# A two-block transformer kernel: stick-breaking attention computed transposed, and products joined around the last norm turns

## The chip, the cores and the metric

The kernel runs on one core of a Trainium2 chip. The metric is the time of one execution on the device in microseconds (us), as the median of three runs. Smaller is better.

## What is computed

The reference is a first block (a state-space and linear-attention mixer with a mixture of experts) on a sequence of 512 rows of width 1024, and behind it a block that is applied twice with different weights (layers l = 0 and 1). The change lies in that second block, all in float32:

```python
h = _rms_norm(x, attn_norm[l]); proj = h @ w_in[l]           # 7328 columns
o_a, o_b = dilated attention, latent attention
o_c = _stick_breaking_attention(c_q, c_k, c_v)                # 8 heads of 64
merged = gates0 * (o_a @ wb_a) + gates1 * (o_b @ wb_b) + gates2 * (o_c @ wb_c)
x = x + merged @ w_out[l]
h2 = _rms_norm(x, mlp_norm[l])
x = x + square(relu(h2 @ w_ff1[l])) @ w_ff2[l]
```

Stick-breaking attention of one head is, with `z` the scaled scores and `strict` the mask key < query:

```python
log_one_minus = where(strict, log_sigmoid(-z), 0.0)
after = cumsum(log_one_minus, reverse=True) - log_one_minus   # over the later keys
weights = exp(where(strict, log_sigmoid(z) + after, -inf))
out = weights @ v
```

So each weight needs the sum of softplus(z) over all keys from its own up to the query.

## The kernel before

Every engine has its own program, written out by hand, and waits on counted semaphores ("lines"). A product of two float32 matrices that must be precise is made of three products of rounded parts (`three`): each operand is split into a high part, written rounded by ScalarE, and a low part, the rest, written by GpSimd (`part_gpsimd`) or VectorE. Helper lines: L229 is every product of TensorE, L232 every transpose, L240 to L256 VectorE's operations, L291 ScalarE's.

A layer of the second block goes through these stages, with a meeting of all four engines (`meet`: each drains, adds to its end line and waits for those of all) between them:

- The norm of x and its turn: per tile of 128 rows ScalarE squares, VectorE scales (`xn`), TensorE turns with 8 transposes (`nturn`), VectorE multiplies with the gain, ScalarE writes the high part and VectorE the low part (`hT`, or `hs` ahead of the feed-forward). For l = 0 this stands at the end of the mixture of experts (`moe_*`), for l = 1 at the end of the feed-forward of l = 0. Then comes a meeting, and only then the first product (`tok a0`).
- An order written by `block2_order`, a list of steps that all engines walk in the same order. Lanes of attention steps are woven with dense products ("filler"). The last piece is the stick stage, between the meetings B and C: 32 units (8 heads by 4 query tiles) in six lanes, five steps each, with the 48 steps of the gate products d = 4 to 7 as filler. A gate step is 6 products of 128x512.
- A unit of the stick stage with `nk` = 128 to 512 keys, queries on the partitions: score on TensorE; scale and mask on VectorE; Abs, Exp, Ln on ScalarE; maximum and addition and then a scan from the last key down on VectorE (L3304); a subtraction on GpSimd (L3709); Exp on ScalarE; `nk`/128 transposes of the weights on TensorE; a copy out of PSUM; the products with v; a copy. GpSimd also writes the low parts of the gate weights (L2620).
- The merge: o_a, o_b, o_c are turned, then for d = 0 to 7 three branch products, sigmoid of the gates (read back from DRAM, `gad`), multiplications and additions on VectorE. SyncE's queue issues in its order: gates 0 and 1, the two output weights (`in_b0o`, 2 MB each), then for each d the branch weights and the gates, each behind a wait. Then the output projection and the norm turns of the feed-forward, a meeting, and the feed-forward (`f1`, `f2`).

## Time and profile before

| | us |
|---|---|
| median of 3 runs | 4967.44 (4967.3 to 4972.65) |
| the profiled execution | 4978.45 |
| its span | 4976.6 |
| TensorE busy | 4460.7 (90%) |
| VectorE, ScalarE, GpSimd busy | 2113.1, 1495.0, 792.0 |
| mean granted clock of TensorE | 0.943 |

A span is the time from the first to the last instruction of the profiled execution. "Idle before" is the time in which an engine did nothing ahead of an instruction, and the arrow names what released it. The granted clock is the share of 2.4 GHz that TensorE had.

### The profile page before, as it was taken

The numbers are of one execution on the slowest core, as the hardware profiler recorded it, in microseconds if no ns is written. First come the engines' busy times: TensorE is split into PE (matmuls) and PEld (weight loads), VectorE is DVE, ScalarE is ACT, GpSimd is POOL, SyncE is SP. The second block draws the span as 40 slices with busy tenths as digits, with TensorE's granted clock in tenths as the row PEclk, the third lists the DMA queues.
The fourth block names the chain that finished last, engine by engine and source line by source line (L and its number), as shares of the span: only waits on it lengthen the run. The fifth ranks groups of instructions, "written<-read, shape, count | busy, mean of one in ns | idle before, by whom it ended". The sixth has DMA issues, their size and how long they took to land. (4 is left out here: it accounts for less than half of the span.)

```text
span 4976.6 us, 90377 instructions
## 1 busy us (share of the span) xinstructions
PE 4460.7 (90%) x38676; PEld 3119.2 (63%) x38676; DVE 2113.1 (42%) x3803; ACT 1495.0 (30%) x2632; POOL 792.0 (16%) x499
## 2 busy tenths in 40 slices
PE   6899899988998899979999798978999988878999
PEld 3566666666555554465443776757788866656787
DVE  2555554554355552131111446354443446345343
ACT  2343333332222221010000334453232334443232
POOL 0021111110132230000000221243000321333000
PEclk9899999988999999989999899989999999999999
DMA  6200000000110123427999311214222211214221
GB/s 228 71 28 11 17 19 17 5 24 16 43 43 29 48 87 131 154 107 302 405 403 411 122 63 50 69 49 168 88 98 77 94 56 48 69 61 154 98 102 51
DMA packets 86824, 512.05 MB, mean 103 GB/s; under 512 B 10504, under 2 KB 11032, under 8 KB 45848
## 3 DMA queue, kind: packets, MB, share of 16 engines
q1 hardware_dynamic: 86424, 506.28, 26.9%
q8 instruction: 305, 5.00, 0.4%
q14 instruction: 95, 0.78, 0.0%
HBM read 476.85 MB, written 29.38 MB: 102 GB/s over the span
## 5 line engine op out<-in xcount | busy, mean ns | idle before, releaser
L229 PE MATMUL ps<-rounded,rounded 128*128 128x512 f32 (+2 forms) x7968 | 1660.4, 367 | 44.3 <-DVE rounded L240 23.7
L229 PEld LDWEIGHTS ps<-rounded,rounded 128*128 128x128 f32 x7968 | 1338.1, 193 | 302.8 <-issue 36.1
L229 PE MATMUL ps<-lower 128*128 128x512 f32 (+10 forms) x4976 | 1075.0, 393 | 56.3 <-issue 22.8
L229 PE MATMUL ps<-upper 64*64 64x64 f32 (+8 forms) x15584 | 834.2, 259 | 152.0 <-DVE upper L268 38.2
L291 ACT ACTIVATE upper<-ps 128x512 f32<-128x512 f32 (+6 forms) x953 | 440.2, 491 | 1671.0 <-PE ps L229 1230.6
L229 PEld LDWEIGHTS ps<-upper 64*64 64x64 f32 (+4 forms) x15584 | 595.7, 145 | 419.8 <-issue 190.6
L229 PEld LDWEIGHTS ps<-lower 128*128 128x128 f32 (+3 forms) x4976 | 576.7, 184 | 442.9 <-issue 376.6
L229 PE MATMUL ps<-lower,upper 64*64 64x64 f32 (+6 forms) x7248 | 607.6, 305 | 47.5 <-DMA lower<-in_ada 20.3
L2620 POOL TENSOR_TENSOR rounded<-lower,rounded 128x1024 fp32r<-128x1024 f32 (+2 forms) x90 | 273.1, 3035 | 1952.3 <-ACT rounded L291 1952.0
L291 ACT ACTIVATE upper<-upper 128x512 f32<-128x512 f32 (+9 forms) x693 | 341.1, 500 | 584.1 <-DVE upper L248 131.4
L229 PEld LDWEIGHTS ps<-lower,upper 64*64 64x64 f32 (+3 forms) x7248 | 334.6, 143 | 258.7 <-issue 198.8
L291 ACT ACTIVATE rounded<-lower 128x2048 fp32r<-128x2048 f32 (+3 forms) x258 | 331.2, 1284 | 413.7 <-PE ps L229 239.4
L268 DVE COPY_PREDICATED upper<-lower,ps 128x256 f32<-128x256 uint8 (+2 forms) x576 | 245.4, 456 | 289.1 <-PE ps L229 259.2
L256 DVE COPY upper<-ps 128x64 f32<-128x64 f32 (+6 forms) x409 | 159.4, 400 | 469.2 <-PE ps L229 383.2
L229 PE MATMUL ps<-upper,lower 128*128 128x128 f32 (+7 forms) x1264 | 347.1, 447 | 6.6 <-DVE lower L248 1.8
L232 PE MATMUL ps<-lower,upper 128*128 128x128 f32 (+1 forms) x1236 | 207.4, 304 | 156.5 <-ACT upper L291 84.1
L240 DVE TENSOR_TENSOR rounded<-lower,rounded 128x2048 fp32r<-128x2048 f32 (+2 forms) x144 | 210.6, 1463 | 224.3 <-ACT rounded L291 223.5
L232 PEld LDWEIGHTS ps<-lower,upper 128*128 128x128 f32 (+1 forms) x1236 | 157.6, 154 | 228.1 <-issue 72.2
L229 PEld LDWEIGHTS ps<-upper,lower 128*128 128x128 f32 (+1 forms) x1264 | 190.3, 201 | 143.1 <-issue 134.1
L240 DVE TENSOR_TENSOR upper<-upper,ps 128x512 f32<-128x512 f32 (+1 forms) x88 | 75.4, 857 | 369.4 <-PE ps L229 365.6
L291 ACT ACTIVATE lower<-ps 128x512 f32<-128x512 f32 (+1 forms) x172 | 101.9, 597 | 341.1 <-PE ps L229 310.9
L240 DVE TENSOR_TENSOR lower<-lower,ps 128x512 f32<-128x512 f32 x164 | 112.7, 687 | 190.5 <-PE ps L229 165.7
(91 smaller groups left out, 2351.0 us busy)
## 6 DMA issues: line engine op xcount, KB each, us to landing
lower<-in_ew SPq DMA_DIRECT2D x140, 1024.0 KB, 10.4
upper<-in_ew SPq DMA_DIRECT2D x52, 1024.0 KB, 13.1
lower<-in_b0f SPq DMA_DIRECT2D x16, 2048.0 KB, 7.4
lower<-in_b1f SPq DMA_DIRECT2D x16, 2048.0 KB, 7.7
upper<-in_ada SPq DMA_DIRECT2D x18, 1024.0 KB, 5.3
lower<-in_wrkv SPq DMA_DIRECT2D x8, 1728.0 KB, 7.3
lower<-in_b0g SPq DMA_DIRECT2D x24, 512.0 KB, 3.8
gad<-upper SPq DMA_DIRECT2D x48, 256.0 KB, 3.8
```

The costliest lines, as they stand in the source:

```text
L229: return self.e.matmul(out, lhsT, rhs, start=start, stop=stop)
L232: return self.e.transpose(out, in_, self.ident[0:n, 0:n])
L240: self.e.tensor_tensor(out, a, b, op).then_inc(line.up(*event), 1)
L256: self.e.tensor_copy(out, a).then_inc(line.up(*event), 1)
L268: self.e.copy_predicated(out, mask, data).then_inc(line.up(*event), 1)
L291: self.e.activation(out, in_, func, bias=bias, scale=scale, accum_out=accum).then_inc(line.up(*event), 1)
L2620: g.e.tensor_tensor(u.low, u.raw, u.high.bitcast(F32), SUB).then_inc(k.parts.pool.up("low", l, key), 1)
```

## The change

1. The stick stage works on whole heads, transposed: keys on the partitions, the ten key-by-query blocks of a head side by side in 1280 columns of three PSUM banks (`BLOCK_AT`, `block_cut`). The mask is a product (an identity times the mask block) added to the scores. ScalarE makes Abs, a copy of the scores, Exp and Ln over 1280 columns, VectorE the loss, ScalarE its high part, VectorE its low part; the sums over the later keys are 20 products with a matrix of -1 and a triangle of -1. VectorE adds them to the kept scores, ScalarE makes Exp, and the 20 products with v need no transposes. Scan, GpSimd's subtraction, the 80 transposes and their copies are gone. Two heads are in work (slots 0 and 1). The scale 0.125 moves into the eviction of c_q.
2. The order of the stick stage is written out: for each head hh the step 0 of hh, step 1 of hh - 1, three gate steps, step 2 (values) of hh - 1, three gate steps (2 and 2, and 3 and 2 at the ends).
3. Low parts of the gate weights that are due behind the meeting B are written by VectorE.
4. TensorE, VectorE and ScalarE leave the meetings ahead of both layers early and wait for them later: TensorE goes from the third turn into the first `tok a0` steps, whose four tiles wait for their own `hT` each, and makes the fourth turn between the two halves of `a0`.
5. Ahead of the feed-forward the first two products run over 384 of the 512 columns around the fourth turn, and over the last 128 behind the meeting.
6. The output weight loads go behind the gates of d = 4 and d = 5.

```diff
-    pe.meet("pe", "moe")
+    k.free = banks.free
...
+        if t == 5:
+            v.leave("dve", "moe")
...
-    drain([lane("stick", 32, 5, z) for z in range(6)], filler, 1.4)
+    for hh, (early, late) in enumerate(((2, 2), *[(3, 3)] * 6, (3, 2), (3, 0))):
+        if hh < 8:
+            out.append(("stick", hh, 0))
+        if hh:
+            out.append(("stick", hh - 1, 1))
+        out += itertools.islice(filler, early)
+        if hh:
+            out.append(("stick", hh - 1, 2))
+        out += itertools.islice(filler, late)
...
-    for n in range(2):
-        fetch(sp, k.wreg[:, 4096 * n:4096 * n + 4096], T[f"b{l}o"][n], f"wo{l}{n}")
     for d in range(2, 8):
         if d > 2:
             branch_load(d)
         gate(d)
+        if d in (4, 5):
+            fetch(sp, k.wreg[:, 4096 * (d - 4):4096 * (d - 4) + 4096], T[f"b{l}o"][d - 4], f"wo{l}{d - 4}")
...
+            if t == "a0" and s % 2 == 0:
+                pe.wait_ge(M.dve, "hT", f"attn{l}", tile)
...
+            if use == ("tok", l, "a0", 0):
+                norm_turn_tensor(k, pe, banks, f"attn{l}", 3, b.scr if l else k.mo.nscr)
```

The stick stage on TensorE:

```diff
+    def stick(hh, s):
...
+        if s == 0:
+            ps = banks.take_at(use, 3 * slot, 3)
+            pe.wait_ge(M.act, "sums", l)
+            for j in (0, 1, 3, 2):
+                pe.mm(ps[:, block_cut(j)], b.ck[e, hh // 2, 128 * j:128 * j + 128], b.cq[e, hh // 2, 128 * j:512], j != 3, False)
+                last = pe.mm(ps[:, BLOCK_AT[j]:BLOCK_AT[j] + 128], b.sums[:, 256:384], b.sums[:, 384:512], False, j != 1)
...
+        if s == 1:
+            pe.wait_ge(team.dve, "parts", l, hh)
+            pe.wait_ge(team.act, "kept", l, hh)
+            for j in (3, 2, 1, 0):
+                for i in range(j, 4):
+                    for part in (b.lost[slot], b.rest[slot]):
+                        last = pe.mm(ps[:, block_cut(j, i)], b.sums[:, 128:256] if i > j else b.sums[:, 0:128],
+                                     part[:, block_cut(i)], j != 1 and i == j and part is b.lost[slot],
+                                     j != 3 and i == 3 and part is b.rest[slot])
...
+        else:
+            pe.wait_ge(team.act, "exp", l, hh)
+            for i in range(4):
+                for j in range(i + 1):
...
+                    for half in (slice(0, 64), slice(64, 128)):
+                        last = pe.mm(ps[half, 1280 + 64 * i:1344 + 64 * i], p[:, half], b.cv[:, j, 64 * hh:64 * hh + 64],
+                                     j == 0, j == i)
```

On VectorE:

```diff
+    def stick(hh, s):
...
+        if s == 0:
+            v.wait_ge(team.act, "log", l, hh)
+            v.stt(t, b.raw[slot], ps[:, 0:1280], 0.0, b.soft[slot], MAX, ADD, "loss", l, hh)
+            v.wait_ge(team.act, "lost", l, hh)
+            v.tt(t, b.rest[slot], b.raw[slot], b.lost[slot].bitcast(F32), SUB, "parts", l, hh)
+        elif s == 1:
+            v.wait_ge(team.pe, "less", l, hh)
+            v.tt(t, b.chance[slot], b.chance[slot], ps[:, 0:1280], ADD, "less", l, hh)
+        else:
+            v.wait_ge(team.pe, "value", l, hh)
+            v.copy(t, b.otC[:, :, 64 * hh:64 * hh + 64], v3(ps[:, 1280:1536], 64), "value", l, hh)
```

On ScalarE:

```diff
+    def stick(hh, s):
...
+        if s == 0:
+            a.wait_ge(team.pe, "score", l, hh)
+            a.act(t, p, ps[:, 0:1280], AF.Abs)
+            a.copy(t, b.chance[slot], ps[:, 0:1280], "kept", l, hh)
+            a.act(t, p, p, AF.Exp, scale=-1.0)
+            a.act(t, p, p, AF.Ln, "log", l, hh, bias=1.0)
+            a.wait_ge(team.dve, "loss", l, hh)
+            a.copy(t, b.lost[slot], b.raw[slot], "lost", l, hh)
+        elif s == 1:
+            a.wait_ge(team.dve, "less", l, hh)
+            a.act(t, b.chance[slot], b.chance[slot], AF.Exp, "exp", l, hh)
```

On TensorE ahead of the feed-forward:

```diff
+    for z in range(2):
+        first(banks.take(("f1", l, 0, z)), 0, z, 0, 384)
+        if z == 0:
+            turn(3)
     pe.meet("pe", ("ffn", l))
```

How the instructions move, at three places. ScalarE in the stick stage of layer 0, before (lanes 0 and 1 carry two heads' units of the same query tile; `rounded_61` is the high part of a gate weight):

```order
L291 ACTIVATE upper<-upper 128x512 [waits lane0_act] x2
L291 ACTIVATE upper<-upper 128x512 [waits lane1_act,lane1_dve]
L291 ACTIVATE upper<-upper 128x512 [waits lane1_act] x2
L291 ACTIVATE rounded_61<-lower 128x1024 [waits parts_act,unit1]
L291 ACTIVATE upper<-upper 128x512 [waits lane0_act,lane0_pool]
L291 ACTIVATE upper<-upper 128x512 [waits lane1_act,lane1_pool]
```

And now, from head 1's first operation (lane 1) to head 0's Exp (lane 0):

```order
L296 ACTIVATE upper<-ps 128x1280 [waits lane1_act,lane1_pe]
L296 ACTIVATE upper<-ps 128x1280 [waits lane1_act]
L296 ACTIVATE upper<-upper 128x1280 [waits lane1_act] x2
L296 ACTIVATE rounded_67<-upper 128x1280 [waits lane1_act,lane1_dve]
L296 ACTIVATE upper<-upper 128x1280 [waits lane0_act,lane0_dve]
```

The Exp of a head, for which its values wait, now stands behind all five operations of the next head.

VectorE at the same place, now (`rounded_69` is the low part of head 1's loss):

```order
L253 SCALAR_TENSOR_TENSOR upper<-ps,upper 128x1280 [waits lane1_dve,lane1_act]
L245 TENSOR_TENSOR rounded_69<-upper,rounded_67 128x1280 [waits lane1_dve,lane1_act]
L245 TENSOR_TENSOR upper<-upper,ps 128x1280 [waits lane0_dve,lane0_pe]
L261 COPY upper<-ps 128x512 [waits proj_dve,stored0,proj_pe]
L261 COPY upper<-ps 128x4x64 [waits lane0_dve,lane0_pe]
```

The addition of head 0's sums stands behind both operations of head 1.

SyncE's queue in the merge, before:

```order
L2888 DMA lower<-gad 128x1536
L490 DMA lower<-in_b0o 128x4096 x2
L2888 DMA lower<-gad 128x1536 [waits main_dve]
L2858 DMA lower<-in_b0br 128x1280 [waits main_pe]
L2888 DMA lower<-gad 128x1536 [waits main_dve]
L2858 DMA lower<-in_b0br 128x1280 [waits main_pe]
```

And now, from the gates of d = 4:

```order
L2937 DMA lower<-gad 128x1536 [waits main_dve]
L504 DMA lower<-in_b0o 128x4096
L2907 DMA lower<-in_b0br 128x1280 [waits main_pe]
L2937 DMA lower<-gad 128x1536 [waits main_dve]
L504 DMA lower<-in_b0o 128x4096
L2907 DMA lower<-in_b0br 128x1280 [waits main_pe]
```

Each output weight load now stands directly ahead of a branch load (those of d = 5 and 6).

## Rows read from the trace of the kernel before

**Rows 1.** The page's part 1: busy time, share of the span, instructions.
```profile
PE 4460.7 (90%) x38676; PEld 3119.2 (63%) x38676; DVE 2113.1 (42%) x3803; ACT 1495.0 (30%) x2632; POOL 792.0 (16%) x499
```

**Rows 2.** Windows, both stick stages: us, busy us (instructions) per engine, PEclk, DMA share, GB/s.
```profile
3214.40:3371.40 157.00, 116.89 (x746) 84.23 (x747) 84.18 (x152) 75.09 (x160) 59.03 (x44) 0.88 0.20 64
4313.40:4471.90 158.50, 118.30 (x747) 85.23 (x747) 84.19 (x152) 75.21 (x160) 59.05 (x44) 0.87 0.20 64
```

**Rows 3.** Groups by line and form, PE, 3214.4 to 3371.4: xcount | busy, mean ns | idle before.
```profile
L232 PE MATMUL ps<-lower,upper 128*128 128x128 f32 x80 | 18.9, 359 | 37.0 <-ACT upper L291 36.5
```

**Rows 4.** Timeline, PE, stick stage of layer 1: start, us, what, xcount [idle before].
```profile
4313.47 1.13 PE L229 MATMUL ps<-upper,lower 64*128 64x512 f32 x4 [0.34 <-PEq L214]
4314.53 1.65 PE L229 MATMUL ps<-rounded,rounded 128*128 128x512 f32 x6
...
4333.40 1.99 PE L229 MATMUL ps<-upper,lower 64*128 64x512 f32 x8
...
4360.00 2.09 PE L229 MATMUL ps<-upper 128*64 128x64 f32 x64
...
4408.08 1.37 PE L232 MATMUL ps<-lower,upper 128*128 128x128 f32 x4 [5.56 <-ACT upper L291]
4409.10 2.91 PE L229 MATMUL ps<-rounded,rounded 128*128 128x512 f32 x6
...
4448.55 22.45 PE L229 MATMUL ps<-rounded,rounded 128*128 128x512 f32 x96
4471.88 1.06 PE L232 MATMUL ps<-lower 128*128 128x128 f32 x8 [0.88 <-DVEq L214]
```

**Rows 5.** Groups by form, PE, 2780 to 4976.
```profile
L229 PE MATMUL ps<-rounded,rounded 128*128 128x160 f32 x192 | 21.7, 274 | 0.0
```

**Rows 6.** Groups by form, ACT, 2780 to 4976.
```profile
L291 ACT ACTIVATE rounded<-lower 128x1280 fp32r<-128x1280 f32 x18 | 22.9, 1272 | 48.0 <-DMA lower<-in_b1br 18.7 <-DMA lower<-in_b0br 17.5 <-DVEq L214 11.5
...
L291 ACT ACTIVATE upper<-upper 128x768 f32<-128x768 f32 x16 | 13.1, 841 | 7.9 <-issue 6.8 <-POOL upper L3698 1.1
...
L291 ACT ACTIVATE upper<-ps 128x768 f32<-128x768 f32 x16 | 12.5, 808 | 33.9 <-PE ps L232 33.7
```

**Rows 7.** Groups by form, DVE, 2780 to 4976.
```profile
L240 DVE TENSOR_TENSOR rounded<-lower,rounded 128x1024 fp32r<-128x1024 f32 x15 | 18.4, 1225 | 11.0 <-ACT rounded L291 10.4
```

**Rows 8.** Timeline, PE, then DVE, end of the experts and start of layer 0.
```profile
2777.61 1.97 PE L232 MATMUL ps<-lower,upper 128*128 128x128 f32 x8 [1.77 <-DVE upper L244]
2784.41 15.78 PE L229 MATMUL ps<-rounded,rounded 128*128 128x256 f32 x118 [4.83 <-DVEq L214]
...
2775.47 1.23 DVE L240 TENSOR_TENSOR rounded<-lower,rounded 128x1024 fp32r<-128x1024 f32 x1
...
2781.70 2.56 DVE L240 TENSOR_TENSOR rounded<-lower,rounded 128x1024 fp32r<-128x1024 f32 x2
```

**Rows 9.** Timeline, PE, end of layer 0 and start of layer 1.
```profile
3870.47 1.09 PE L232 MATMUL ps<-lower 128*128 128x128 f32 x8 [1.11 <-DVE lower L244]
3875.55 1.94 PE L232 MATMUL ps<-lower 128*128 128x128 f32 x8 [3.99 <-DVE lower L244]
3881.31 18.87 PE L229 MATMUL ps<-rounded,rounded 128*128 128x256 f32 x136 [3.81 <-DVEq L214]
```

**Rows 10.** Timeline, PE, then DVE, ahead of the feed-forward of layer 0.
```profile
3504.72 1.97 PE L232 MATMUL ps<-lower 128*128 128x128 f32 x8 [5.18 <-DVE lower L244]
3510.45 19.74 PE L229 MATMUL ps<-rounded,rounded 128*128 128x512 f32 x75 [3.76 <-DVEq L214]
...
3501.93 1.22 DVE L240 TENSOR_TENSOR rounded<-lower,rounded 128x1024 fp32r<-128x1024 f32 x1 [1.12 <-ACT rounded L291]
```

**Rows 11.** Timeline, PE, DVE, ACT, merge of layer 1.
```profile
4548.15 12.25 PE L229 MATMUL ps<-rounded,rounded 128*128 128x512 f32 x42 [11.12 <-DVE rounded L240]
...
4534.28 4.18 DVE L240 TENSOR_TENSOR upper<-lower 128x512 f32<-128x512 f32 x1
...
4510.00 1.27 ACT L291 ACTIVATE rounded<-lower 128x1280 fp32r<-128x1280 f32 x1 [3.54 <-DMA lower<-in_b1br]
```

More of the change, by code:

```diff
@@ L214, in leave, with join @@
         self.e.drain().then_inc(self.k.end[mine].up(stage), 1)
+    def join(self, stage):
+        for e in self.k.end:
+            self.wait_ge(self.k.end[e], stage)
     def meet(self, mine, stage):
         self.leave(mine, stage)
-        for e in self.k.end:
-            self.wait_ge(self.k.end[e], stage)
+        self.join(stage)
 class TensorPort(Port):
@@ L311, in take, with take_at @@
         self.i = i + n if i + n < self.hi else self.lo
+        for b in range(i, i + n):
+            assert self.free.get(b, ()) is not None, "no bank is free"
+            if self.free.get(b):
+                self.pe.wait_ge(*self.free[b])
+            self.free[b] = None
+        self.pe.k.bank[use] = (i, n)
+        return self.pe.k.ps[:, 512 * i:512 * (i + n)]
+    def take_at(self, use, i, n):
         for b in range(i, i + n):
@@ L2351, in moe_tensor @@
     combine(7)
-    for i in range(4):
+    pe.leave("pe", "moe")
+    for i in range(3):
         norm_turn_tensor(k, pe, banks, "attn0", i, b.nscr)
-    pe.meet("pe", "moe")
+    k.free = banks.free
 def moe_vector(k, v):
@@ L2542, in block2_map @@
     b.cq, b.ck, b.cv = v3(RB[:, 0:2048], 512), v3(RD[:, 0:2048], 512), v3(RC[:, 0:2048], 512)
-    b.on = RC[:, 2048:2560]
-    b.trip = [RA[:, 1536 * z:1536 * z + 1536] for z in range(6)]
+    at = ROUNDED + 4096
+    b.soft = [k.plain(at + 3840 * z, 1280) for z in range(2)]
+    b.chance = [k.plain(47272 + 1280 * z, 1280) for z in range(2)]
+    b.lost = [k.rounded(at + 3840 * z + 1280, 1280) for z in range(2)]
+    b.raw = [k.plain(at + 3840 * z + 2560, 1280) for z in range(2)]
+    b.rest = [k.rounded(at + 3840 * z + 2560, 1280) for z in range(2)]
+    b.sums = k.rounded(43176, 512)
     up = ROUNDED + 4808
@@ L2557, in block2_map @@
     b.order = block2_order()
+    end = b.order.index(("meet", "B"))
+    for key in (step[1] for step in b.order[end:] if step[0] == "part"):
+        b.units[key].late = True
     return b
@@ L2614, in part_scalar, with part_done, part_vector @@
     a.act(k.parts.act, u.high, u.raw, AF.Copy, "high", l, key)
+def part_done(k, l, key):
+    return k.parts.dve if k.b2[l].units[key].late else k.parts.pool
+def part_vector(k, v, l, key):
+    u = k.b2[l].units[key]
+    if u.late:
+        v.wait_ge(k.parts.act, "high", l, key)
+        v.tt(k.parts.dve, u.low, u.raw, u.high.bitcast(F32), SUB, "low", l, key)
 def part_gpsimd(k, g, l, key):
     u = k.b2[l].units[key]
+    if u.late:
+        return
     g.wait_ge(k.parts.act, "high", l, key)
@@ L2993, in block2_tensor @@
     b, M, P, tail = k.b2[l], k.main, k.proj, k.tail
-    free = {}
+    free = k.free
     whole, pb, banks = Banks(pe, 0, 8, free), Banks(pe, 6, 8, free), Banks(pe, 0, 6, free)
+    pe.join(("block2", 0) if l else "moe")
     at = {}
@@ L3003, in dense @@
             at["ps"] = pb.take(use)
-            pe.wait_ge(k.parts.pool, "low", l, key)
+            pe.wait_ge(part_done(k, l, key), "low", l, key)
         if name == "tok":
@@ L3036, in attend @@
             pe.mm(ps[:, 0:o.nk], o.query, o.key, True, True).then_inc(L.pe.up(*use), 1)
-            banks.give(use, L.dve, "score" if stick else "max", *o.u)
-        elif s == (3 if stick else 2):
+            banks.give(use, L.dve, "max", *o.u)
+        elif s == 2:
             use = ("turn", *o.u)
@@ L3044, in attend @@
             last.then_inc(L.pe.up(*use), 1)
-            banks.give(use, L.dve if stick and o.i % 2 else L.act, *use)
-        elif s == (4 if stick else 3):
+            banks.give(use, L.act, *use)
+        elif s == 3:
             use = ("value", *o.u)
             ps = banks.take(use)
-            pe.wait_ge(L.dve if stick and o.i % 2 else L.act, "turn", *o.u)
+            pe.wait_ge(L.act, "turn", *o.u)
             n = o.nk // 128
@@ L3142, in block2_tensor, with first @@
                 turn(i - 1)
-    turn(3)
+    def first(ps, h, z, n0, n1):
+        for kk in range(8):
+            last = three(pe, ps[:, n0:n1], both(b.wr[h % 2], lambda p: v3(p, 256)[:, kk, 128 * z:128 * z + 128]),
+                         both(b.hs, lambda p: p[:, kk, n0:n1]), kk == 0, kk == 7)
+        return last
+    pe.wait_ge(M.dve, "lo", l, 0)
+    pe.wait_ge(M.dve, "hs", l, 2)
+    for z in range(2):
+        first(banks.take(("f1", l, 0, z)), 0, z, 0, 384)
+        if z == 0:
+            turn(3)
     pe.meet("pe", ("ffn", l))
@@ L3148, in block2_tensor @@
             h = 8 * q + z2
-            w = b.wr[h % 2]
             for z in range(2):
                 use = ("f1", l, h, z)
-                ps = banks.take(use)
-                pe.wait_ge(M.dve, "lo", l, h)
-                for kk in range(8):
-                    last = three(pe, ps, both(w, lambda p: v3(p, 256)[:, kk, 128 * z:128 * z + 128]), both(b.hs, lambda p: p[:, kk, :]),
-                                 kk == 0, kk == 7)
+                if h:
+                    ps = banks.take(use)
+                    pe.wait_ge(M.dve, "lo", l, h)
+                    last = first(ps, h, z, 0, 512)
+                else:
+                    last = first(k.pair(use), h, z, 384, 512)
                 last.then_inc(M.pe.up(*use), 1)
```

122 lines of the change are left out of this document (53 added, 69 removed).

## The prediction

> **What bounds the kernel.** I read the page's busy times first: TensorE is busy 90% of the span, no other engine half of it [rows 1], so time can only be won where TensorE stands still, runs at half its clock, or does products that can go. Then I read the windows of the stages. The two stick stages last 157.0 and 158.5 us with TensorE busy 117 and 118 and a granted clock of 0.88 and 0.87 [rows 2]; 37.0 us of the first are idle time ahead of the transposes, which wait for ScalarE's Exp [rows 3]. The other places are small: 4.83 and 3.81 us ahead of the first product of each layer [rows 8, 9], 5.18 and 3.76 around the last turn ahead of each feed-forward [rows 10], 11.12 us ahead of the output projection [rows 11]. In the timeline the reader is to see what such a wait costs beyond itself: after 5.56 us without work six 128x512 products take 2.91 us where six take 1.65 otherwise [rows 4]. That is the clock at its level of 1.2 GHz in place of 2.4.
>
> **Prices for the stick stage.** An unrounded product leaves two records, so rows x4 and x8 hold two and four scores. Between 1.13 us for four records and 1.99 for eight lie 0.215 us per record of 512 columns [rows 4]. A head now has 1280 score columns, two records each: 1.07 us. Its four mask products are 128 wide; the nearest row is 160 wide, 21.7/192 = 0.113 us each [rows 5]: 0.45. They alternate with the scores, and a change of kind costs: the four records lasted 1.06 us from their start to that of the next kind, not 0.86 [rows 4]. Seven or eight such changes at 0.15 make 1.2. A head's scores: 2.7 us (1.5 if changes were free). The Trainium skill, "TensorE: Matmul & The Clock Gate", Back-to-back issue gap, gives about 81 ns for a product of 128 columns in a stream with its weight load; by it the masks would be 0.1 us per head cheaper and the whole 2 us lower. Here the 0.113 row decides, since it holds this kernel's rounded operands.
>
> The sums of a head are 20 rounded products: two of 512 columns at 22.45/96 = 0.234 [rows 4], four of 384 at 0.176 and six of 256 at 0.117 by their columns, eight of 128 at 0.113: 2.8 us. The values are 40 records; 64 take 2.09 us [rows 4], so 1.3, with a change of kind 1.45. Three gate steps (18 products) with a change of kind are 4.36 us, two are 2.96. All of TensorE's work for a head beside the filler is thus 7 us.
>
> ScalarE: 768 columns take 0.808 from PSUM and 0.841 from SBUF, 1280 take 1.272 [rows 6], so 0.84 ns per column. Abs and the kept copy of 1280 are 1.24 each, Exp and Ln 1.27 each: 5.0. VectorE: 1024 columns take 1.225 [rows 7], 1280 about 1.5. A hand-over is 0.05 (two dependent operations of 1.225 last 2.56 together, 0.11 more than their sum [rows 8]).
>
> **The chain of a head.** From Abs of head h to the Exp of head h - 1 everything is in one line, because ScalarE and VectorE take head h first: 5.0 (four passes), 1.5 (loss), 1.27 (high part), 1.5 (low part of h), 1.5 (addition of h - 1), 1.27 (Exp of h - 1), seven hand-overs: 12.4 us. TensorE meanwhile has the sums of h - 1 and three gate steps, 7.2 us, and then stands still for about 5.5 us. Then come in series the values 1.45, three gate steps 4.36, the scores of h + 1 2.7, and 0.3 until ScalarE sees them: 21.2 us per head at full clock. The idle 5.5 us are as long as the 5.56 of [rows 4], so I add the half clock. It costs at least 1.27 there (the six products) and by the row before it (four transposes in 1.37, where eight of the next kind take 1.06) about as much again; I take 2.1, with 0 and 2.8 as bounds. **A head then takes 23.3 us.**
>
> The stage: 1.2 (four copies of 128 columns, 0.3 each by the slope of [rows 6]) + 2.7 + 0.3 gives Abs of head 0 at 4.2. ScalarE is free of it after 5.0 + 1.5 + 1.27 + 0.15 and then has two gate weights (1.06 each by the slope): Abs of head 1 at 14.3, its follower at 14.3 + 23.3 = 37.6, head 7 at 154.1. Values of head 6 at 166.5; they, two gate steps and the slow clock end at 173.0, the sums of head 7 at 175.8, three gate steps at 180.2, its values at 181.6, and the meeting (0.88 [rows 4]) at 182.5. **Against 157.0 and 158.4 that is 25.5 and 24.1 longer, 49.6 together.** The stage breaks even at some 20.2 us per head. What is removed gives little back on this path: the transposes' 18.9 us [rows 3] were paid, but the sums cost 22, and GpSimd's 59 us [rows 2] were never TensorE's. VectorE's eleven low parts (1.225 each [rows 7]) stand where it waits for values, and cost nothing while the 5.5 us of slack per head is there; without it each would add its own length.
>
> **The joins.** Into layer 0: the low part of tile 0 ended at 2776.7 [rows 8], so two tiles (48 products at 15.78/118 = 0.134) run until 2783.1, then the fourth turn, until 2784.6. VectorE's multiplication for it and then the low part of tile 2 stand behind that turn, 1.23 each: tile 2 from 2787.2, tile 3 until 2793.6, against 2784.4 + 96 x 0.134 = 2797.3. I take 3 us won. Into layer 1 the low part of tile 2 stands ahead of that: from 3872.1 (the third turn and 0.5 for a drain) two tiles of 24 x 0.139 [rows 9] and the turn end at 3879.9, tile 2 at 3883.2, tile 3, which waits for its low part until 3883.5, at 3886.8, against 3881.3 + 13.3 = 3894.6: 8 won. Feed-forward: tile 2 is there at 3503.15 [rows 10]; 24 products of 384 (0.176) with the slow clock end at 3509.5, the turn at 3510.6, the other 24 at 3514.8 (tile 3 comes at about 3514.3), and 48 of 128 columns at 0.113 at 3520.3, against 3510.45 + 48 x 19.74/75 = 3523.1: 3 per layer. **Together 17 us won.** If the first tiles wait for something else the gain is 0.
>
> **The output weights.** ScalarE waits for each branch load (3.54 us at d = 5 [rows 11]); with 2 MB directly ahead of two of them these come later. That moves ScalarE's sigmoids, but TensorE is some 3 us ahead of need. The 11.12 us stand behind VectorE's additions, 4.18 us for one [rows 11], which this move does not touch. I take 1 us lost per layer, with -3 and +5 as bounds.
>
> **Sum.** 49.6 - 17 + 2 = +34.6 us on the profiled 4978.45. That execution is 0.22% above the median of 4967.44; I put the change on the median: **5002 us**.
>
> **Rivals.**
> (a) The clock stays up. The transposes, which are TensorE's coldest rows (359 ns each [rows 3]), are gone and a head's products come in fuller stretches. Then 14 heads save 2.1 us: 5002 - 29 = 4973, no change that a measurement tells (about 0.2%, 10 us). Against it: 5.5 us idle each time.
> (b) Faster: the scores' changes of kind cost nothing (the masks' weights load under the scores), and the clock stays. A head then takes 21.2 - 1.4 = 19.8, both stages end about level with before, and the joins remain: 4973 - 23 = 4950. It decides from under about 21 us per head, where the loss of the stages is smaller than the joins' 17. For it: TensorE's weight loads overlap elsewhere. Against: the 1.06 us of [rows 4].
> (c) The late output weights hold a branch load so long that TensorE waits: +5 per layer in place of 1: 5010.
> (d) The joins do nothing, since the first tile's wait comes last anyway: 5019.
>
> **Chances.** Forecast with (c) and (d), slower: 0.62 (0.48, 0.08, 0.06). (a) and its neighbours, within 0.2%: 0.16. (b), faster: 0.22, a good part of it for a chain shorter than its rows say. Range 4945 to 5030: it takes in (b), and above the half clock at its bound of 2.8 per head (+10) with (c) and (d) in part. The slower case's own range is 4980 to 5030.
>
> **What would show it.** The stick stages at 182 us each, Abs of one head to Abs of the next 23 us apart, TensorE idle 5 us ahead of each head's values, released by ScalarE, and a granted clock under 0.9 there. The first f32 products of a layer no longer wait for a drain. Wrong if TensorE's longest wait in the stage is under 3 us, if the heads are under 21 us apart, or if the waits ahead of the output projection have changed by more than 5 us.

## The result, and the profile after

| | before | after |
|---|---|---|
| median, us (4 runs of each, side by side) | 4967.37 (4964.47 to 4972.65) | 5046.97 (5039.65 to 5055.19) |
| ratio, with its 95% interval | | 1.0156 (1.0143 to 1.0168) |
| profiled execution, its span, us | 4978.45, 4976.6 | 5047.68, 5045.9 |
| stick stage, layer 0 and 1, us | 156.9, 158.4 | 193.5, 194.4 |
| end of the stick stage to the output projection, us | 75.1, 76.3 | 81.9, 82.1 |
| output projection of layer 0 to the stick stage of layer 1, us | 867.0 | 856.9 |
| output projection of layer 1 to the end, us | 428.5 | 423.5 |

The change is slower by 80 us where 35 were forecast, outside the range. The stages of the two profiled executions account for 69.3 us: 36.6 and 36.0 in the stick stages, 6.8 and 5.8 in the merges, less 10.1 and 5.0 in the stretches with the joins, less 0.7 ahead of all of them. The rest of the 80 is that the profiled execution of before stood 11 us above its median, and the one of after 0.7; where those 11 us lay the traces don't tell. The start of the first stick stage alone moves between 3197 and 3223 us among kernels with nothing changed ahead of it but, at most, the join. So from here on stages are compared by their lengths, and whole times by the ratios to the kernel before on the same chip (0.001 is 5 us). Each length is that of one trace, and a stage that an edit leaves alone moves too: the stick stage of layer 1 lasts 158.4 us in the kernel before and 155.6 in e12_oldstick, which has the same one. A difference of under 3 us in a single stage is thus not told apart from none.

A stick stage is taken from its first score product to the first transposes behind it. In the changed kernel TensorE stands still for 1.53 us directly ahead of that first product, until ScalarE has written the four matrices of 128 columns for masks and sums; before, it was 0.34. These 1.2 us per layer count in the stretch ahead of the stage, so the stages are 1.2 us longer, and the joins won 1.2 us more, than their stretches say.

TensorE's busy time grew by 72 us, although transposes are gone (page, part 1, after, against [rows 1]):

```profile
PE 4532.8 (90%) x38996; PEld 3188.3 (63%) x38996; DVE 2066.7 (41%) x3601; ACT 1494.5 (30%) x2448; POOL 672.6 (13%) x411
```

Windows of both stick stages after (columns as in [rows 2]). GpSimd does nothing there any more, the granted clock fell from 0.88 and 0.87 to 0.84 and 0.82:

```profile
3213.70:3407.20 193.50, 154.10 (x858) 116.24 (x858) 56.72 (x51) 73.21 (x63) 0.00 (x0) 0.84 0.15 50
4346.00:4540.40 194.40, 157.38 (x858) 118.78 (x859) 56.73 (x51) 73.21 (x64) 0.00 (x0) 0.82 0.15 50
```

One head on TensorE, timeline of the stage in layer 0 (start, us, what, count, idle before), and the stage's end:

```profile
3247.47 1.12 PE L234 MATMUL ps<-lower,upper 64*128 64x512 f32 x2
3248.52 0.33 PE L234 MATMUL ps<-rounded 128*128 128x128 f32 x1
3248.78 0.91 PE L234 MATMUL ps<-lower,upper 64*128 64x384 f32 x2
3249.61 0.33 PE L234 MATMUL ps<-rounded 128*128 128x128 f32 x1
...
3251.33 5.77 PE L234 MATMUL ps<-rounded,rounded 128*128 128x128 f32 x32
3263.76 2.40 PE L234 MATMUL ps<-upper 128*64 128x64 f32 x40 [6.66 <-ACT upper L296]
3266.10 4.73 PE L234 MATMUL ps<-rounded,rounded 128*128 128x512 f32 x18
3270.76 1.12 PE L234 MATMUL ps<-lower,upper 64*128 64x512 f32 x2
...
3390.91 1.39 PE L234 MATMUL ps<-upper 128*64 128x64 f32 x40
3392.22 14.14 PE L234 MATMUL ps<-rounded,rounded 128*128 128x512 f32 x60
3407.24 1.06 PE L237 MATMUL ps<-lower 128*128 128x128 f32 x8 [0.87 <-DVEq L215]
```

The scores of a head run from 3247.47 to 3251.33, 3.86 us. Behind them come the 20 sums and two gate steps (x32), then 6.66 us idle until ScalarE's Exp, then the values at half clock (2.40 us with a granted clock of 0.50; the last head's take 1.39 with 1.00), three gate steps in 4.7 us where they take 4.4 at full clock (e1_order), and the next scores. And behind the last values 60 gate products are left over: 14.1 us in which no attention work is left to hide them. The stage of layer 1 ends in the same way. ScalarE's timeline for this head, its last operation being the Exp of the head before:

```profile
3251.53 2.52 ACT L296 ACTIVATE upper<-ps 128x1280 f32<-128x1280 f32 x2 [3.36 <-PE ps L234]
3254.08 2.58 ACT L296 ACTIVATE upper<-upper 128x1280 f32<-128x1280 f32 x2
3258.21 1.27 ACT L296 ACTIVATE rounded<-upper 128x1280 fp32r<-128x1280 f32 x1 [1.56 <-DVE upper L253]
3262.44 1.27 ACT L296 ACTIVATE upper<-upper 128x1280 f32<-128x1280 f32 x1 [2.96 <-DVE upper L245]
```

From the end of the scores (3251.33) to the start of the values (3263.76) are 12.43 us; of the values of heads 1 to 6, five start 12.43 us behind the scores and one 12.46. The chain itself, from the start of Abs (3251.53) to the end of the Exp (3263.71), is 12.18 of these.

The merge after. TensorE and ScalarE in layer 0, and SyncE's issues. The branch loads of d = 5 and 6 are issued right behind the 2 MB of an output weight each; ScalarE waits 8.23 and 5.82 us for them, where it waited 3.55 and 3.47 before ([rows 11] has such a wait in layer 1), and TensorE waits for GpSimd's low parts in the middle of the products, where before it did so only once, for 2.1 us at their start, as it still does. In layer 0 these waits are 3.4 us of the merge's 6.8; the same 210 products also take 52.2 us in place of 48.9, with a granted clock of 0.81 behind the first of the waits. In layer 1 it is one wait of 4.68 us. The wait ahead of the output projection is what it was ([rows 11]). The last line is layer 1's:

```profile
3454.57 8.70 PE L234 MATMUL ps<-rounded,rounded 128*128 128x512 f32 x30 [2.87 <-POOL rounded L3342]
3463.83 14.07 PE L234 MATMUL ps<-rounded,rounded 128*128 128x512 f32 x60 [0.55 <-POOL rounded L3342]
...
3489.09 35.14 PE L234 MATMUL ps<-rounded,rounded 128*128 128x512 f32 x144 [11.20 <-DVE rounded L245]
...
3450.28 1.27 ACT L296 ACTIVATE rounded<-lower 128x1280 fp32r<-128x1280 f32 x1 [8.23 <-DMA lower<-in_b0br]
...
3459.47 1.27 ACT L296 ACTIVATE rounded<-lower 128x1280 fp32r<-128x1280 f32 x1 [5.82 <-DMA lower<-in_b0br]
...
3439.75 0.43 SPq L504 DMA_DIRECT2D lower<-in_b0o  x1
3440.23 0.43 SPq L2907 DMA_DIRECT2D lower<-in_b0br  x1
...
4588.31 22.56 PE L234 MATMUL ps<-rounded,rounded 128*128 128x512 f32 x90 [4.68 <-POOL rounded L3342]
```

The join into layer 1 (against [rows 9]). The wait of 3.81 us is gone, the fourth turn lies between the halves of `a0`, and a new wait of 2.33 us stands behind: the low part of the next unit, which GpSimd writes (L2660), is late now. From the start of the third turn to the next transposes of another kind (456 products and the fourth turn lie between) it is 59.9 us where it was 66.9: 6.9 won.

```profile
3909.12 1.06 PE L237 MATMUL ps<-lower 128*128 128x128 f32 x8 [1.20 <-DVE lower L249]
3910.55 5.85 PE L234 MATMUL ps<-rounded,rounded 128*128 128x256 f32 x48 [0.37 <-PEq L215]
3916.23 1.04 PE L237 MATMUL ps<-lower 128*128 128x128 f32 x8
3917.03 3.08 PE L234 MATMUL ps<-rounded,rounded 128*128 128x256 f32 x24
3920.99 3.07 PE L234 MATMUL ps<-rounded,rounded 128*128 128x256 f32 x24 [0.88 <-DVE rounded L245]
3926.38 13.85 PE L234 MATMUL ps<-rounded,rounded 128*128 128x256 f32 x115 [2.33 <-POOL rounded L2660]
```

The join into layer 0 (against [rows 8]) won less: 64.9 us where it was 65.6. TensorE now waits twice for VectorE's low parts, and the first 48 products take 8.3 us, with a granted clock of 0.66, in place of the 6.4 that the forecast gave them:

```profile
2773.39 1.97 PE L237 MATMUL ps<-lower,upper 128*128 128x128 f32 x8 [3.24 <-DVE upper L249]
2776.36 8.47 PE L234 MATMUL ps<-rounded,rounded 128*128 128x256 f32 x48 [1.00 <-DVE rounded L245]
2784.67 1.04 PE L237 MATMUL ps<-lower,upper 128*128 128x128 f32 x8
2788.41 50.07 PE L234 MATMUL ps<-rounded,rounded 128*128 128x256 f32 x408 [2.70 <-DVE rounded L245]
```

### The profile page after: what moved, and what is told of

Its sections match the earlier page's. It is cut to its first block and busy times, and to the rows that moved or that the text cites. A ratio compares the mean times of both kernels' runs of the same rounds, so it can differ in the third digit from the quotient of the medians.

```text
span 5045.9 us, 90165 instructions
## 1 busy us (share of the span) xinstructions
PE 4532.8 (90%) x38996; PEld 3188.3 (63%) x38996; DVE 2066.7 (41%) x3601; ACT 1494.5 (30%) x2448; POOL 672.6 (13%) x411
## 5 line engine op out<-in xcount | busy, mean ns | idle before, releaser
L234 PE MATMUL ps<-rounded,rounded 128*128 128x512 f32 (+3 forms) x8384 | 1719.4, 365 | 53.7 <-DVE rounded L245 37.6
L296 ACT ACTIVATE upper<-ps 128x512 f32<-128x512 f32 (+7 forms) x953 | 469.5, 520 | 1771.7 <-PE ps L234 1338.6
L234 PE MATMUL ps<-lower,upper 64*64 64x64 f32 (+7 forms) x7376 | 662.2, 309 | 50.8 <-DMA lower<-in_ada 20.1
L234 PEld LDWEIGHTS ps<-lower,upper 64*64 64x64 f32 (+4 forms) x7376 | 355.2, 145 | 270.4 <-issue 206.0
L2660 POOL TENSOR_TENSOR rounded<-lower,rounded 128x1024 fp32r<-128x1024 f32 (+2 forms) x68 | 217.2, 3195 | 1855.0 <-ACT rounded L296 1462.6
L296 ACT ACTIVATE rounded<-lower 128x2048 fp32r<-128x2048 f32 (+4 forms) x266 | 333.4, 1255 | 431.9 <-PE ps L234 239.4
L296 ACT ACTIVATE upper<-upper 128x768 f32<-128x768 f32 (+11 forms) x485 | 286.2, 593 | 526.1 <-DVE upper L269 115.3
L245 DVE TENSOR_TENSOR rounded<-lower,rounded 128x512 fp32r<-128x512 f32 (+2 forms) x166 | 237.5, 1431 | 248.4 <-ACT rounded L296 247.3
L234 PE MATMUL ps<-upper,lower 128*128 128x512 f32 (+2 forms) x1136 | 320.9, 442 | 5.9 <-DVE lower L253 1.8
L261 DVE COPY upper<-ps 64x256 f32<-64x256 f32 (+7 forms) x329 | 135.7, 422 | 377.1 <-PE ps L234 331.0
L234 PEld LDWEIGHTS ps<-upper,lower 128*128 128x128 f32 x1136 | 178.7, 202 | 132.0 <-issue 125.2
L237 PE MATMUL ps<-lower,upper 128*128 128x128 f32 (+1 forms) x1076 | 167.4, 294 | 80.3 <-DVE upper L249 40.2
```

What stands on the lines that cost most here:

```text
L234: return self.e.matmul(out, lhsT, rhs, start=start, stop=stop)
L237: return self.e.transpose(out, in_, self.ident[0:n, 0:n])
L245: self.e.tensor_tensor(out, a, b, op).then_inc(line.up(*event), 1)
L261: self.e.tensor_copy(out, a).then_inc(line.up(*event), 1)
L296: self.e.activation(out, in_, func, bias=bias, scale=scale, accum_out=accum).then_inc(line.up(*event), 1)
L2660: g.e.tensor_tensor(u.low, u.raw, u.high.bitcast(F32), SUB).then_inc(k.parts.pool.up("low", l, key), 1)
```

## The experiments

Twelve kernels; e12_oldstick is an edit of the kernel before, the others are edits of the changed kernel. Their stage lengths, read as above, and their ratios to the kernel before (us; "middle" is from the output projection of layer 0 to the stick stage of layer 1, "end" from the output projection of layer 1 on):

| kernel | stick 0, 1 | merge 0, 1 | middle | end | ratio (95%) |
|---|---|---|---|---|---|
| before | 156.9, 158.4 | 75.1, 76.3 | 867.0 | 428.5 | 1 |
| after | 193.5, 194.4 | 81.9, 82.1 | 856.9 | 423.5 | 1.0156 (1.0143 to 1.0168) |
| e1_order | 155.5, 155.6 | 80.7, 81.3 | 856.1 | 422.8 | 1.0003 (0.9994 to 1.0012) |
| e2_weights | 195.3, 195.4 | 76.3, 75.8 | 854.8 | 423.7 | 1.0133 (1.0118 to 1.0148) |
| e3_count | 197.6, 195.9 | 81.5, 83.0 | 855.8 | 425.0 | 1.0168 (1.0153 to 1.0183) |
| e4_nojoin | 195.3, 193.5 | 80.7, 81.4 | 865.7 | 428.0 | 1.0180 (1.0163 to 1.0197) |
| e5_warm | 185.9, 184.3 | 81.3, 82.5 | 857.6 | 423.2 | 1.0103 (1.0089 to 1.0117) |
| e6_grouped | 186.2, 186.0 | 80.3, 81.6 | 856.5 | 425.5 | 1.0115 (1.0101 to 1.0129) |
| e7_count1 | 188.7, 188.1 | 82.2, 81.7 | 857.3 | 425.2 | 1.0135 (1.0120 to 1.0151) |
| e8_joint | 153.5, 154.4 | 76.2, 76.7 | 857.3 | 424.8 | 0.9966 (0.9952 to 0.9979) |
| e9_same | 201.7, 200.1 | 80.4, 81.1 | 856.2 | 423.0 | 1.0175 (1.0160 to 1.0190) |
| e10_other | 193.5, 195.1 | 81.3, 82.1 | 856.7 | 424.9 | 1.0163 (1.0143 to 1.0182) |
| e11_best | 141.6, 141.6 | 76.3, 76.5 | 850.5 | 423.1 | 0.9908 (0.9894 to 0.9923) |
| e12_oldstick | 157.2, 155.6 | 75.0, 75.0 | 855.0 | 424.8 | 0.9966 (0.9951 to 0.9981) |

### The order of the heads

```diff
+        if hh:
+            out.append(("stick", hh - 1, 1))
         if hh < 8:
             out.append(("stick", hh, 0))
-        if hh:
-            out.append(("stick", hh - 1, 1))
```

> The changed kernel with one swap in its stick stage: the sums, the addition and the Exp of head h - 1 stand ahead of the first operations of head h, on all engines. Theory A (the chain Abs(h) to Exp(h - 1), 12.4 us, stands in series with the values, the late gates and the scores, and its idle time halves the clock): the chain from the sums to the values is then only 2.8 + 1.5 + 1.3 us and lies under the scores of h and the early gates; a head takes about 15.5 to 16.5 us in place of 23.0, TensorE waits less than 1 us ahead of the values, the granted clock in the stage is above 0.95, and the time falls by some 45 us per layer, 90 in all. Theory B (TensorE's own work in the stage is what is long: the scores with their changes of kind, the 20 sums): a head stays above 20 us and the time falls by 20 us or less.

Measured: a head takes 16.5 us (3304.48 to 3320.98 below), both stages together are 76.8 us shorter, and the ratio falls from 1.0156 to 1.0003, that is 76 us. The longest waits in layer 0 are now 4.7 us ahead of head 0's sums and 2.5 ahead of head 7's; ahead of values there is none. TensorE's timeline of this kernel:

```profile
3293.39 2.99 PE L234 MATMUL ps<-rounded,rounded 128*128 128x128 f32 x20 [0.87 <-DVE rounded L245]
...
3304.48 1.39 PE L234 MATMUL ps<-upper 128*64 128x64 f32 x40
...
3320.98 1.39 PE L234 MATMUL ps<-upper 128*64 128x64 f32 x40
```

Theory A holds, with a size smaller than its 90: the granted clock is 0.91 in this stage, not above 0.95. The same instructions in another order are 77 us apart, so the order in which the engines take the heads is worth more than the whole 73 us that the stages had lost, and the transposed form as such need not be slower. The swap is made on all engines at once; that it acts through ScalarE's and VectorE's order is read from the chain, not tested engine by engine. With the order alone the change would have been level with the kernel before.

### The output weights

```diff
+    for n in range(2):
+        fetch(sp, k.wreg[:, 4096 * n:4096 * n + 4096], T[f"b{l}o"][n], f"wo{l}{n}")
     for d in range(2, 8):
...
-        if d in (4, 5):
-            fetch(sp, k.wreg[:, 4096 * (d - 4):4096 * (d - 4) + 4096], T[f"b{l}o"][d - 4], f"wo{l}{d - 4}")
```

> The changed kernel with the two output weight loads back ahead of the loop over d. Theory A (the late output weights hold the branch loads of d = 5 and 6, whose high and low parts TensorE then waits for): the waits for GpSimd's low parts in the merge (2.9 and 0.6 us in layer 0, 4.7 in layer 1) go, the merge is 6 us shorter in layer 0 and 5 in layer 1, and the time falls by 11 to 13 us. Theory B (the merge is longer for another reason, for instance because the branch loads ahead of the merge begin later against the stick stage's end): the time falls by less than 3 us.

Measured: the merges are 5.5 and 6.3 us shorter and as long as before, TensorE has no wait inside them but the one at their start, and the ratio falls by 0.0023, 11 us. Theory A holds. The late loads won nothing in return: the wait ahead of the output projection is 12.41 us in layer 0 of this kernel and 11.20 with them.

### The filler

The list that the steps are taken from holds the low parts (`part`) as items too, so `islice(filler, 3)` is often two gate steps and a low part. Counting gate steps alone:

```diff
+    def take(n):
+        while n:
+            out.append(next(filler, ("end",)))
+            n -= out[-1][0] != "part"
...
-        out += itertools.islice(filler, early)
+        take(early)
```

> The changed kernel with gate steps alone counted as filler in the stick stage: a list item that is a low part no longer takes the place of a gate step, so that the 14 us of gate products behind the last head's values go into the loop. Theory A: about half of these ten steps stand in the idle time ahead of the values and cost nothing there, the others add 1.4 us each on the path: 7 us less per layer, 14 in all, and 3 to 5 us idle ahead of each values remain. Theory B (the idle time moves with them, because the values' release comes later too, as VectorE and ScalarE evict more gates ahead of it): no change, within 4 us.

Measured: 4.1 and 1.5 us more per stage in place of 7 less, ratio 1.0168, which its interval doesn't tell from the changed kernel's: neither theory. The last late gate steps do end with the values now. But look at the start of the stage in this kernel:

```profile
3222.76 6.87 PE L234 MATMUL ps<-rounded,rounded 128*128 128x512 f32 x18
3233.95 2.90 PE L234 MATMUL ps<-rounded,rounded 128*128 128x512 f32 x6 [4.32 <-DVE rounded L245]
3236.78 2.07 PE L234 MATMUL ps<-lower,upper 64*128 64x512 f32 x2
```

The fourth gate step waits for a low part that VectorE writes behind head 0's own operations; head 1's scores stand behind it, 19.9 us after head 0's, where the changed kernel has 9.8. That gave a cleaner run, e7_count1, which counts from head 1 on only.

> As e3_count, but the four list items of the first group as in the changed kernel; gate steps alone are counted from head 1 on. In e3_count the loop from head 0's values to head 7's became 7.0 us longer and the tail 14.1 shorter, as Theory A there had it, and what undid it was the start: the fourth gate step of the first group waited 4.3 us for a low part that stands behind head 0's work on VectorE, and head 1's scores came 13 us later. Theory A (that is all): the start is as in the changed kernel, the stage some 5 us shorter than there, the time 8 to 14 us under the changed kernel's. Theory B (a gate step in the loop costs more than its 1.4 us): the time is that of the changed kernel or more.

Measured: 188.7 and 188.1 us, 4.8 and 6.3 less than in the changed kernel, and 10 us less by the ratio. Theory A holds. This is also the stage as the prediction assumed it, with all gate steps in the loop; it was to last 182.5 us, and counted from the meeting on, as there, it lasts 189.9. TensorE now stands still 3.7 us ahead of most values, and the half clock falls on the values in some heads and behind them in others (values 1.39, then 18 gate products in 6.0 us where they take 4.4); from values to values it is 24.1 us on average.

### The scores

```diff
             for j in (0, 1, 3, 2):
                 pe.mm(ps[:, block_cut(j)], b.ck[e, hh // 2, 128 * j:128 * j + 128], b.cq[e, hh // 2, 128 * j:512], j != 3, False)
+            for j in (0, 1, 3, 2):
                 last = pe.mm(ps[:, BLOCK_AT[j]:BLOCK_AT[j] + 128], b.sums[:, 256:384], b.sums[:, 384:512], False, j != 1)
```

> The changed kernel with the four unrounded score products of a head first and its four rounded mask products behind them, in place of alternating. Theory A (of the 3.9 us of a head's scores, the changes of kind cost 0.15 to 0.2 us each; six of eight go): 0.9 to 1.2 us less per head on the path, 14 to 19 us in all. Theory B (the 3.9 us are the unrounded products themselves, at 0.84 us per 512 columns, and the masks' own time): less than 0.3 us per head, under 5 us in all.

Measured: a head's scores last 2.85 us (3241.67 to 3244.52) in place of 3.86, the stages are 7.3 and 8.4 us shorter, the ratio is 20 us lower. The two stages account for 15.7 of these 20. So a change between the unrounded 64-row products and the rounded 128-row ones costs 1.01/6 = 0.17 us, as the prediction had it (0.15). TensorE's timeline:

```profile
3241.67 2.42 PE L234 MATMUL ps<-lower,upper 64*128 64x512 f32 x8
3244.03 0.66 PE L234 MATMUL ps<-rounded 128*128 128x128 f32 x4
```

But then the 3.86 us still hold 1.2 us more than the 2.7 forecast, and they lie in the unrounded products: 2.4 us for 1280 columns, where 1.07 had been read from [rows 4]. Two runs add one such product ahead of the head's scores, with the head's own operands or with those of the other head of its pair:

```diff
+            e2 = e        # e9_same; e10_other: slice(64 - 64 * slot, 128 - 64 * slot)
+            pe.mm(ps[:, 1024:1536], b.ck[e2, hh // 2, 0:128], b.cq[e2, hh // 2, 0:512], True, True).then_inc(team.pe.up("extra", l, hh), 1)
             for j in (0, 1, 3, 2):
+                if j == 3:
+                    pe.wait_ge(team.pe, "extra", l, hh)
```

> The changed kernel with one more unrounded product of 64x512 directly ahead of each head's scores, with the operands of the head itself (the same 64 partitions), into columns that are overwritten later; TensorE waits for it ahead of the third score. Theory A (an unrounded product of 512 columns takes 0.84 us when its neighbour uses the same 64 partitions; the 0.43 us per score that the prediction read from the kernel before hold only where two heads' scores, one on partitions 0 to 63 and one on 64 to 127, stand side by side and run at once): 0.8 to 0.9 us more per head on the path, 13 to 15 us in all. Theory B (0.43 us per product wherever it stands, and the rest of the 3.9 us is the changes of kind): 6 to 8 us in all.

> As e9_same, but the added product has the operands of the other head of the pair (the other 64 partitions). Theory A (the two halves of the array run at once): with the head's own first score beside it, it adds 0.1 to 0.25 us per head, 2 to 4 us in all, some 10 less than e9_same. Theory B: the same time as e9_same.

The added product and the first score, in e9_same:

```profile
3295.53 1.98 PE L234 MATMUL ps<-lower,upper 64*128 64x512 f32 x4
3297.44 0.33 PE L234 MATMUL ps<-rounded 128*128 128x128 f32 x1
```

and in e10_other:

```profile
3294.64 1.13 PE L234 MATMUL ps<-lower,upper 64*128 64x512 f32 x4
3295.70 0.33 PE L234 MATMUL ps<-rounded 128*128 128x128 f32 x1
```

Two products of 512 columns last 1.91 us to the next kind on the same 64 partitions, and 1.06 on different ones, as long as one alone does (1.05). The stages together are 13.9 us longer in e9_same and 0.7 in e10_other. Theory A holds in the timelines and the stages; the whole times are weaker evidence, 9 and 3 us above the changed kernel's by the ratios, with intervals that overlap each other and its own, where 13 to 15 and 2 to 4 were expected. The 1.06 us of e10_other are those of [rows 4] to the hundredth: what had been read there were two heads' scores at once. The Trainium skill, "TensorEngine Tiling (Array Packing)", Key Properties, says that different tiles of the array can work in parallel, and this trace agrees (1.06 us for two). The Trainium skill says in the same place that a change of the tiling mode drains the engine, with which the 0.17 us agree in kind (the runs don't separate the mode from the change of type).

### The clock

e5_warm makes the products of one gate step per head four times over, ahead of the wait for the Exp. What those gates hold is then not the reference's.

```diff
+        if 0 < hh < 8:
+            z = max(z for z, step in enumerate(out) if step and step[0] == "gate" and step[3] < 3)
+            out[z + 1:z + 1] = [("again", *out[z][1:])] * 3
```

> The changed kernel in which one gate step per head, ahead of the wait for the Exp, makes its six products four times instead of once (18 more products, 4.2 us at full clock; what these gates hold is no longer right, the values are). The idle time of 3.7 to 6.7 us ahead of each head's values is thus filled with work that nobody needs. Theory A (the idle time halves the clock, and that costs some 2.2 us per head in the values and in the gate steps behind them): the values take 1.4 us everywhere, 12 gate products behind them 2.8 to 3.0 in place of 3.5 to 5.0, a head takes some 2 us less, and with its 14 us more of work per 7 heads off the path the time falls by 20 to 30 us. Theory B (the slow products behind the wait have another cause, such as evictions that lag): no gain, and up to 10 us more where the idle time is shorter than the added work.

Measured: with 126 products more per stage, the stages are 7.6 and 10.1 us shorter, and the ratio is 26 us lower; the stages account for 17.7 of these, and 9.0 lie ahead of the first stage (it starts at 3204.7 in place of 3213.7), where nothing was changed. Where the added work leaves about 1 us of idle time the values take 1.39 us and the head 20.6 (3321.72 to 3342.31, granted clock 1.00); the changed kernel's same head took 22.9 (3333.26 to 3356.16, granted 0.87). Where 2.5 us are left, the clock has fallen again (granted 0.50 during those values). TensorE's timeline of this kernel:

```profile
3321.72 1.39 PE L234 MATMUL ps<-upper 128*64 128x64 f32 x40 [1.05 <-ACT upper L296]
3323.03 3.05 PE L234 MATMUL ps<-rounded,rounded 128*128 128x512 f32 x12
...
3342.31 1.39 PE L234 MATMUL ps<-upper 128*64 128x64 f32 x40 [1.12 <-ACT upper L296]
...
3362.89 2.40 PE L234 MATMUL ps<-upper 128*64 128x64 f32 x40 [2.51 <-ACT upper L296]
```

Theory A holds, though not for every head's values as it expected: the half clock behind the idle time costs 2.3 us in such a head. Set against full-clock prices, the changed kernel's heads 0 to 5 in layer 0 lose 1.3 to 2.8 us each to it, some 1.9 on average. The gain of this run over all heads is less than 2.3 each, since some keep 2.5 us of idle time and the first ones are delayed by the added work.

### The joins

e4_nojoin takes parts 4 and 5 out of the changed kernel (its edit is the change's, turned round), e12_oldstick puts them alone into the kernel before.

> The changed kernel without parts 4 and 5 of the change: full meetings ahead of both layers with the fourth turn ahead of them, and the first feed-forward products behind the meeting over all 512 columns. Theory A: the joins won 2 us into layer 0, 6 to 7 into layer 1 (9 less the 2.3 us in which TensorE now waits for a low part), and 3 per feed-forward: 14 us more. Theory B (the joins only move the waits): no more than 3 us.

> The kernel before with parts 4 and 5 of the change alone (the joins): stick stage, low parts and output weights as before. Theory A (the joins are worth what e4_nojoin showed): 14 to 16 us less than before, 4952 to 4954, ratio 0.997. Theory B (they win only beside the changed stage's order): within 4 us of before.

Measured: without them the middle is 8.8 us longer and the end 4.6, the ratio 0.0024 higher (12 us); alone in the kernel before, the middle is 12.1 shorter, the end 3.7, and the ratio 0.9966, 17 us. Theory A holds in both. The joins are worth 12 to 17 us whatever the stick stage does; of e12_oldstick's 17, up to 3 lie in a stick stage that its edit doesn't touch. What they win ahead of layer 0 is 0.7 us between the kernel before and the changed one (1.5 between the changed one and e4_nojoin), under what the spans can tell.

### All of it together

> The order of e1_order, the weights' place of e2_weights and the counting of e7_count1 together. Theory A (the three costs are apart): a head takes 16.8 us, by TensorE's own work, the waits of about 1 us ahead of each head's sums are filled by gate steps, the 14 us behind the last values go down to 4 or less: 8 us per layer under e1_order, 11 for the weights: 4940 to 4948, 0.4 to 0.55% under the kernel before. Theory B (with the filler in the loop the waits only move): 4955 to 4960.

> e8_joint with the grouped scores of e6_grouped. e8_joint came out at 0.9966 of the kernel before, not 0.9946: its merges are as short as in the kernel before, but its stick stage is 153.5 us long, only 2 under e1_order's. Theory A (its heads, 17.4 us on average, are TensorE's own work plus up to 1.7 us in which a gate waits for an eviction): the 0.8 us that grouping takes off each head's scores comes off the stage, 13 us in all: 4938 to 4945. Theory B (its heads are bound by the evictions and the chain on VectorE): under 4 us less than e8_joint.

e8_joint (the edits of e1, e2 and e7) came out at 0.9966, 4955 us: its merges are right, but its stages only 2.0 and 1.2 us under e1_order's, although the 14 us of filler are gone from their ends: Theory B was nearer, and single lengths don't tell these 2.0 and 1.2 us from nothing. e11_best adds the grouped scores and falls by 12 and 13 us per stage, twice what Theory A expected, to **4924.5 us, 0.9908 (0.9894 to 0.9923) of the kernel before**. Windows of layer 0, e8_joint:

```profile
3210.60:3364.10 153.50, 144.41 (x859) 106.88 (x859) 55.89 (x51) 73.72 (x64) 0.00 (x0) 0.91 0.19 63
```

and e11_best:

```profile
3212.50:3354.20 141.70, 129.24 (x859) 101.10 (x860) 55.71 (x51) 73.54 (x64) 0.00 (x0) 0.95 0.20 68
```

TensorE is idle 9 and 12 us of these; the difference is its busy time, 15 us, with 0.91 against 0.95 of the clock. Six changes of kind fewer per head are 8 us of it; the rest, by subtraction, is the clock's. In e8_joint 18 gate products take 5.96 us (granted clock 0.71) in one head and 4.38 (1.00) in others without an idle time of 2 us anywhere near; with grouped scores they take 4.35 or 4.36 in every head. That the changes of kind are what lowers the clock is suggested by this and was not tested by itself; in e6_grouped, where the idle times are still there, grouping moved the granted clock of the stage only from 0.84 to 0.85.

## Why the prediction was wrong

- **The chain.** Right: 12.4 us forecast from Abs to the end of the Exp, 12.18 measured, and 12.43 from the scores to the values, for which the forecast had 12.7; released by ScalarE in every head, and e1_order shows that the order is its cause. One term is luckier than its source: the row behind the hand-over shows 0.11 us, not the 0.05 taken, which would make the chain 12.8; the hand-overs of this chain measure 0.03 to 0.05.
- **The half clock.** Right: 2.1 us per head taken, 2.3 measured in a head whose idle time was filled (e5_warm), some 1.9 on average. Only at the stage's start was it left out: head 0's scores take 5.3 us there, with a granted clock of 0.67. Rival (a) fell: the granted clock in the stages was 0.84 and 0.82.
- **The scores, 2.7 us.** The first step that failed. It took 0.215 us per record of 512 columns from [rows 4], without asking whose products these were: two heads' on the two halves of the partitions, side by side. A head alone on its half pays twice, and the 2.7 are 3.86. The term that was off is the 1.07, not that of the masks. In the stage with all gate steps in the loop (e7_count1: 189.9 us from the meeting on, against 182.5) eight times 1.16 is more than the whole difference; the shorter chain gave some of it back.
- **The 48 gate steps fit in the loop.** The second step that failed. The diff says `islice(filler, 3)`, and the filler holds low parts as well; so ten steps stayed over, 14.1 us at the end of each stage. They are missing in the loop, which is why a head took 23.0 us and not the 24.1 of e7_count1 (forecast 23.3), so the net error is what e7_count1 shows: 4.8 and 6.3 us. A forecast that agrees per head can hide two errors of opposite sign; counting the products between two scores in the order would have shown it.
- **Output weights, 1 us lost per layer.** Rival (c)'s mechanism was the true one, and it is larger than its 5: 5.5 and 6.3 us (e2_weights). The step that failed is "TensorE is some 3 us ahead of need": ScalarE's wait for the load of d = 5 grew by 4.7 us, and that was more than the lead: TensorE waited 2.87 us there.
- **The joins, 17 us won.** Right in sum, and in part by luck: 15.8 in the stretches of the two traces, 12 to 17 by e4_nojoin and e12_oldstick. By the rows it is 0.7 us into layer 0 where 3 were forecast (the lower clock on the first products, and waits for low parts), 6.9 into layer 1 where it was 8, and about 3 ahead of a feed-forward, as forecast. Into layer 1, 2.3 us went into a wait for GpSimd's next low part, which the forecast left out.
- **The sum.** 34.6 forecast; the stick stages add 23.0 to that (72.6 against 49.6), the merges 10.6, the joins 1.2: 69.4, the 69.3 of the two spans. (With the 1.2 us per layer put where the forecast had them, the stages add 25.4 and the joins take off 1.2; the sum is the same.) The break-even of 20.2 us per head doesn't follow from its own stage sum, which gives 19.2 to 19.8; the sum doesn't use it. The range stopped at 5030 because it bounded the clock and the rivals, and neither of the two counts that were wrong.

## What to carry to other kernels

When two items are in work on shared engines, put the short end of the older one ahead of the long beginning of the newer one: the same instructions were 77 us apart by that alone. Before a price is taken from a row, ask what ran beside it, since two 64-row products on different halves of TensorE cost as much as one; and before a loop is said to hold its filler, count the filler's items as the order prints them. A layout that needs two kinds of product in turns should group them.

## What was not expected of the hardware

- Beside another on its own 64 partitions an unrounded 64x512 product adds 0.86 us (1.91 for two, 1.05 for one), and beside one on the other 64 it adds 0.01 us (1.06 for two).
- Two megabytes directly ahead of a branch load lengthened ScalarE's wait for it from 3.55 to 8.23 us (layer 0, d = 5).
- The granted clock was 0.91 in a stage in which TensorE stood idle for 9 us of 153.5, and 0.95 with 12 idle of 141.7 and fewer changes of kind. What lowers it in the first is open.
